# A two-block decoder on one core: low-part products one tile later, one weight split moved, sums of squares on 64 columns

## The chip, the cores and the metric

The kernel runs on one NeuronCore of a Trainium2 chip. The metric is device time in microseconds: the median over three runs of the kernel, 1620.4 us (1619.64 to 1622.11).

## What is computed

The reference takes 256 tokens `x` and 256 context tokens, each of width 1024, through two blocks of two layers.

- First block. Layer 0: RMS norm with a gain and shift from an adaptive vector (`ada`), differential attention (8 heads), residual; norm, up-projection to 2 x 2816, a depthwise convolution over three positions, SiLU gate, down-projection, residual. Tokens and context go through it, 512 rows in all. Layer 1: the same with neighbourhood attention; its FFN has the 256 tokens alone. A norm closes the block.
- Second block, two hybrid layers on the 256 tokens: a norm, one projection `w_in`, and four branches (a sparse attention with compressed keys, a pooling mixer, a short convolution, an attention with forgetting), gated and merged; a last norm.

```python
def rmsnorm(t, g):
    tf = t.astype(jnp.float32)
    tf = tf * lax.rsqrt(jnp.mean(tf * tf, axis=-1, keepdims=True) + NORM_EPS)
    return tf.astype(t.dtype) * g
...
def nsa_compress(k, pos_emb, w1, b1, w2, b2):
    ...
    blocks = k[:, idx] + pos_emb
    flat = blocks.reshape(B, nc, NSA_CMP_LEN * hd)
    return jax.nn.silu(flat @ w1 + b1) @ w2 + b2
```

## The kernel before

**Products in three parts.** Activations lie with the features on the partitions, in 8 tiles of 128 (`DT`), and 512 or 256 tokens in the free dimension. Each large product is made exact enough from split operands: an operand is a high part in the round format (`WH`, `NH`) and the low rest (`WL`, `NL`), and for each tile k of the contraction TensorE does high x high, high x low and low x high into one PSUM sum (`mm3`, L551 to L553).

**Weights.** `wstream` holds them in units of 128 x 2048. SP loads a unit into one of three `RAW` buffers; ACT copies the high part (`split_hi`, L523), in two halves; DVE, and for some second halves POOL, subtract it from the raw weights (`split_lo`, L533). All that is done two units ahead of TensorE's use: `ahead(key)` names the unit that is split while unit `key` is used. TensorE waits for the low half that holds its tile (`wait_weights`).

**Order of the work.** Each engine has one program written out by hand, as a list of steps (`pe_...`, `act_...`, `dve_...`, `pool_...`), and the engines meet at semaphores that count up. There is no scheduler: what an engine does stands in the order of the code.

**A norm** n (0 and 2 ahead of the attentions of layers 0 and 1, 1 and 3 ahead of their FFNs, 5 and 6 in the hybrid layers, 7 the last) goes like this. ACT squares a tile of `X` (L696); POOL adds the first six squares up (L716), for all norms but 0 and 5; `pe_sums` (L718 to L733) sums over the partitions: the square is the stationary operand, in groups of 128 tokens, and a column of ones `ONE` the moving one (L731). Each product is one column, the sum of squares of 128 tokens, one token per partition. In norm 5 the moving operand is the two columns of `GSQ`. One such product is two passes in the trace, as every product of plain f32. In all, 42 products have the moving `ONE` and 16 have `GSQ`, the trace's x84 and x32. DVE makes the mean (`dve_mean`, L784), POOL the root (L794), TensorE spreads it over the partitions (`pe_rs_rows`, L801), and then tile after tile: DVE scales (L828), ACT adds the shift and rounds, which is the high part (L844), and DVE (even tiles, L856) or POOL (odd tiles, after one more ACT step, L848 and L869) makes the low part. Meanwhile TensorE does products of the adaptive vectors (`pe_ada`, L565), whose 32-column stationary operands come straight from `RAW`.

**The first unit behind a norm** is where TensorE meets the normalized tiles as they come. For tile 0, `pe_high_first` (L902 to L912) does the two products with the high operand for both output halves j (L908, L909), waits for the low part, and does the third (L912). Tiles 1 to 7 then go through `pe_wide(..., abreast=True)` or, in FFN 1 where both output halves share a bank, through `pe_tiles` (L958 to L960): for each tile it waits for the low part first (`pe_wait_norm`) and then does all six products. This holds behind norms 1, 2 and 3. Norm 0 and the hybrid layers' norms have other code.

**The compression** (`pe_compress_up`, L2082 and L2083) takes two units of weights, 16 tiles each, one for keys and one for values; between them it turns the forget gates' `LF` (L2088). The low part of the first unit's first half is DVE's step `lo_prep(e, l, "kf", False)` in `dve_head`. It stands between the two parts of the rotation of the keys: `dve_turn_product` (a shuffle L1958 and a product L1960) and `dve_turn_sum` (L1967). The second halves of both units are POOL's.

Of the kernel before, what the change touches and what calls it, by code (L numbers as in the profile page):

```python
# [9 lines left out]
ALU = mybir.AluOpType  # L10
# [351 lines left out]
def bass_two_block_decoder(nc, wstream, first, small, consts, late, rpb, xin, out):  # L362
    ctx = ExitStack()
    with ctx:
# [353 lines left out]
        def pe_sums(e, n, m):  # L718
# [10 lines left out]
            width = 2 if n == 5 else 1  # L729
            for q in range(NORM_T[n] // P):  # L730
                mm = e.matmul(NB[:, width * q:width * q + width], t[:, q * P:q * P + P], GSQ[:, m, :] if n == 5 else ONE,  # L731
                              start=first and q == 0, stop=m == DT - 1, skip_group_check=True)
# [40 lines left out]
        def dve_mean(e, n):  # L773
# [4 lines left out]
            if n == 5:  # L778
                for kind in range(2):
                    mm = e.tensor_scalar(MS[:, 2 * kind:2 * kind + 2], NB[:, 0:4].rearrange("p (q s) -> p s q", s=2)[:, kind, :],  # L780
# [3 lines left out]
            e.tensor_scalar(MS[:, 0:nt], NB[:, 0:nt], 1.0 / D, EPS, ALU.mult, ALU.add).then_inc(ms_done, 1)  # L784
# [117 lines left out]
        def pe_high_first(e, n, key, outs, T, shared):  # L902
            v, wh, wl = weights(key)
            wait_weights(e, v, 0)
            e.wait_ge(n_hi, split_base(n) + NORM_T[n] // 256)
            for j, o in enumerate(outs):
                w = slice(P * j, P * j + P)
                e.matmul(o, wh[:, 0, w], NH[:, 0, 0:T], start=j == 0 or not shared, stop=False, skip_group_check=shared)  # L908
                e.matmul(o, wl[:, 0, w], NH[:, 0, 0:T], start=False, stop=False, skip_group_check=shared)  # L909
            pe_wait_norm(e, n, 0)  # L910
            for j, o in enumerate(outs):
                e.matmul(o, wh[:, 0, P * j:P * j + P], NL[:, 0, 0:T], start=False, stop=False, skip_group_check=shared)  # L912

        def pe_wide(e, key, outs, T, xh, xl, wait_x, abreast=False):
# [3 lines left out]
            if abreast:  # L918
                for k in range(1, nk):
                    wait_weights(e, v, k)  # L920
                    wait_x(k)
                    for j, o in enumerate(outs):
                        mm = mm3(e, o, wh[:, k, P * j:P * j + P], wl[:, k, P * j:P * j + P], xh[:, k, 0:T],
                                 xl[:, k, 0:T], False, k == nk - 1)
                        if k == nk - 1:
                            mm.then_inc(gemm, 1)
                return
# [2431 lines left out]
```

## Time and profile before

| | |
|---|---|
| three runs | 1619.64, 1620.4, 1622.11 us (median 1620.4) |
| the profiled execution: its own time | 1614.25 us |
| its span | 1612.1 us |
| mean granted TensorE clock | 0.996 |
| TensorE / its weight load / DVE / ACT / POOL busy | 98% / 83% / 59% / 48% / 34% |
| chain that ended last, by engine | TensorE 89%, DVE 6%, ACT 2% |
| DMA | 249.26 MB, 155 GB/s |

The profile is one execution. An engine's busy share is its time with an instruction in it; a TensorE product in it shows the time from its start to its modelled end, some 0.28 to 0.5 us, while the next may start much sooner, so the pace is read from the starts. The granted clock is the share of TensorE's full 2.4 GHz that it was given. "Idle before" with a releaser names what an engine waited for.

### The profile page before, as it was taken

The page shows a single profiled execution, that of the slowest core. Times are in us where ns is not written, and L with a number is a line of the kernel's source. Part 1 is how long each engine was busy: PE and PEld are TensorE (multiplying, and loading weights), DVE is VectorE, ACT ScalarE, POOL GpSimd, SP SyncE. Part 2 cuts the span into 40 slices and gives each one's busy share as a digit, 9 for nine tenths or more (in the row PEclk, how much of TensorE's full clock was granted, in tenths as well). Part 3 has the DMA queues.
Part 4 walks back from the last instruction along what each step waited for, and adds up shares of the span by engine and source line. Part 5 has one row for each costly group of instructions (what it writes and reads, how often), then busy time and mean ns, then how long its engine had stood idle before and what let it go on. Part 6 is the DMA issues. An engine that isn't in the chain of part 4 may idle for free.

```text
span 1612.1 us, 24595 instructions
## 1 busy us (share of the span) xinstructions
PE 1584.4 (98%) x9838; PEld 1339.2 (83%) x9838; DVE 949.9 (59%) x1485; ACT 767.5 (48%) x1410; POOL 548.8 (34%) x358
## 2 busy tenths in 40 slices
PE   8999999999999999999999999999999999999998
PEld 5778557778887888879767999999999989999987
DVE  4334485555564653343275888658776567768545
ACT  5323585444322443243274755445544555564454
POOL 2224243322211222123172111016334567533564
PEclk9999999999999999999999999999999999999999
DMA  9264500434174222364314654445534544533451
GB/s 394 83 250 186 228 9 27 183 138 164 48 282 165 83 76 81 140 209 157 104 28 163 238 187 168 169 170 183 182 131 158 183 160 170 185 128 134 180 203 58
DMA packets 52464, 249.26 MB, mean 155 GB/s; under 512 B 20608, under 2 KB 20736, under 8 KB 25856
## 3 DMA queue, kind: packets, MB, share of 16 engines
q1 hardware_dynamic: 43600, 243.90, 41.9%
q10 hardware_dynamic: 8752, 3.80, 1.0%
q8 instruction: 78, 1.28, 0.3%
q14 instruction: 34, 0.28, 0.0%
HBM read 246.63 MB, written 1.05 MB: 154 GB/s over the span
## 4 chain that ended last, share of the span: by engine, by line
PE 89%; DVE 6%; ACT 2%; issue 1%; DMA 1%; POOL 0%; SPq 0%; ACTq 0%; POOLq 0%; DVEq 0%
PE psq L551 14%; PE psq L553 14%; PE psq L552 14%; PE psq L965 7%; PE ps L551 6%; PE ps L553 6%; PE ps L552 6%; PE psq L966 4%; PE ps L965 3%; PE ps L565 2%; PE ps L966 1%; DVE WL L533 1%; PE psq L1373 1%; PE ps L1401 1%; DMA RAW<-wstream 1%
## 5 line engine op out<-in xcount | busy, mean ns | idle before, releaser
L533 POOL TENSOR_TENSOR WL<-RAW,WH 128x1024 fp32r<-128x1024 f32 (+2 forms) x116 | 304.4, 2626 | 504.5 <-ACT WH L523 493.4
L533 DVE TENSOR_TENSOR WL<-RAW,WH 128x1024 fp32r<-128x1024 f32 (+3 forms) x264 | 329.2, 1272 | 235.6 <-ACT WH L523 235.4
L523 ACT ACTIVATE WH<-RAW 128x1024 fp32r<-128x1024 f32 (+2 forms) x380 | 361.0, 1001 | 156.2 <-DMA RAW<-wstream 92.5
L551 PE MATMUL psq<-NHL,WH 128*128 128x256 f32 (+1 forms) x1260 | 410.2, 326 | 3.3 <-POOL NHL L869 1.8
L553 PE MATMUL psq<-NHL,WL 128*128 128x256 f32 (+1 forms) x1260 | 404.3, 321 | 0.0
L552 PE MATMUL psq<-NHL,WH 128*128 128x256 f32 (+1 forms) x1260 | 404.2, 321 | 0.0
L551 PEld LDWEIGHTS psq<-NHL,WH 128*128 128x128 f32 x1260 | 239.9, 190 | 32.4 <-issue 7.6
L553 PEld LDWEIGHTS psq<-NHL,WL 128*128 128x128 f32 x1260 | 239.9, 190 | 17.8
L552 PEld LDWEIGHTS psq<-NHL,WH 128*128 128x128 f32 x1260 | 240.0, 191 | 16.6
L965 PE MATMUL psq<-NHL,WH 128*128 128x512 f32 x416 | 148.6, 400 | 0.0
L551 PE MATMUL ps<-NHL,WH 128*128 128x256 f32 (+1 forms) x368 | 122.1, 332 | 0.0
L552 PE MATMUL ps<-NHL,WH 128*128 128x256 f32 (+1 forms) x368 | 121.2, 329 | 0.0
L553 PE MATMUL ps<-NHL,WL 128*128 128x256 f32 (+1 forms) x368 | 121.2, 329 | 0.0
L966 PE MATMUL psq<-NHL,WL 128*128 128x256 f32 x416 | 116.7, 280 | 0.0
L965 PEld LDWEIGHTS psq<-NHL,WH 128*128 128x128 f32 x416 | 78.2, 188 | 20.1 <-issue 0.7
L1727 DVE SCALAR_TENSOR_TENSOR TMP<-psq,SMALL,TMP 128x510 f32<-128x510 f32 (+1 forms) x64 | 39.2, 613 | 80.5 <-ACT TMP L1688 80.4
L696 ACT ACTIVATE TMP<-X 128x256 f32<-128x256 f32 (+1 forms) x52 | 25.1, 497 | 122.6 <-DVE X L1540 60.0
L1688 ACT ACTIVATE TMP<-psq,SMALL 128x512 f32<-128x512 f32 (+1 forms) x64 | 40.8, 666 | 87.7 <-PE psq L553 87.6
L966 PEld LDWEIGHTS psq<-NHL,WL 128*128 128x128 f32 x416 | 78.5, 189 | 0.0
L551 PEld LDWEIGHTS ps<-NHL,WH 128*128 128x128 f32 x368 | 69.7, 189 | 10.2 <-issue 3.3
L553 PEld LDWEIGHTS ps<-NHL,WL 128*128 128x128 f32 x368 | 69.7, 189 | 6.4
L552 PEld LDWEIGHTS ps<-NHL,WH 128*128 128x128 f32 x368 | 69.7, 190 | 6.0
(398 smaller groups left out, 2871.0 us busy)
## 6 DMA issues: line engine op xcount, KB each, us to landing
RAW<-wstream SPq DMA_DIRECT2D x196, 1024.0 KB, 4.9
RAW<-wstream SPq DMA_DIRECT2D x32, 704.0 KB, 4.0
K<-first SPq DMA_DIRECT2D x4, 1024.0 KB, 17.1
X<-xin SPq DMA_DIRECT2D x2, 1024.0 KB, 6.3
V<-first SPq DMA_DIRECT2D x2, 1024.0 KB, 19.2
Q<-first SPq DMA_DIRECT2D x2, 1024.0 KB, 25.4
BR<-rpb ACTq DMA_DIRECT2D x8, 256.0 KB, 7.9
BR<-rpb SPq DMA_DIRECT2D x8, 256.0 KB, 8.6
```

The source lines that it names most:

```text
L523: e.activation(WH[:, u % 3, a:z], RAW[:, v % 3, a:z], ACT.Copy).then_inc(w_hi, 1)
L533: e.tensor_tensor(WL[:, u % 3, a:z], RAW[:, v % 3, a:z], WH[:, u % 3, a:z].bitcast(F32), ALU.subtract).then_inc(w_lo_p if pool else w_lo_v, 1)
L551: e.matmul(o, lh, rh, start=start, stop=False)
L552: e.matmul(o, lh, rl, start=False, stop=False)
L553: return e.matmul(o, ll, rh, start=False, stop=stop)
L565: mm = e.matmul(AB[32 * j:32 * j + 32, :], CB[:, c, :], RAW[:, v % 3, 512 * j:512 * j + 512], start=k == 0, stop=k == ada_units(b) - 1)
L696: e.activation(sq_tile(n, m), X[:, m, 0:NORM_T[n]], ACT.Square).then_inc(x_sq, 1)
L965: e.matmul(o[:, 0:512], wh, x, start=start, stop=False, skip_group_check=True)
L966: return e.matmul(o[:, 0:256], wl, x[:, 0, :], start=False, stop=stop, skip_group_check=True)
L1373: e.matmul(bank[2 * (p % 2) + e2][:, :], Q[1][ps, m, qt * P:qt * P + P], K[1][ps, m, :], start=True, stop=True).then_inc(att_qk, 1)
L1688: e.activation(acc_tile(l, U, s), up_banks(l, jj)[s][:, :], ACT.Identity, scale=small_at("fconv", (3 * l + 1) * 44 + j + FT * s), bias=sma ...
L1727: e.scalar_tensor_tensor(out=a3[:, :, 1:256], in0=o3[:, :, 0:255], scalar=w(0), in1=a3[:, :, 1:256], op0=ALU.mult, op1=ALU.add).then_inc(u ...
```

## The change

Three edits, all in the order or the shape of instructions that were there.

1. `pe_high_first` now does the whole unit. For each k it does the two products with the high operand for tile k and then the one with the low operand for tile k - 1, so low parts are waited for one tile later. High parts are waited for at each tile. The number of products is the same.
2. In `dve_head`, `lo_prep(e, l, "kf", False)` stands ahead of the memset of `CM` and of `dve_turn_product`.
3. In `pe_sums`, the moving operand is 64 columns: the one column of ones read 64 times, or in norm 5 each of the two columns read 32 times. Each group of 128 tokens has its own 64 columns in PSUM, and `dve_mean` reads one of each group (one of each 32 in norm 5). Norm 0 has its own code and stays.

```diff
@@ pe_sums
-            width = 2 if n == 5 else 1
+            if n == 5:
+                kinds = GSQ[:, m, :].unsqueeze(2).to_broadcast([P, 2, 32])
+            else:
+                kinds = ONE.to_broadcast([P, 64])
             for q in range(NORM_T[n] // P):
-                mm = e.matmul(NB[:, width * q:width * q + width], t[:, q * P:q * P + P], GSQ[:, m, :] if n == 5 else ONE,
+                mm = e.matmul(NB[:, 64 * q:64 * q + 64], t[:, q * P:q * P + P], kinds,
                               start=first and q == 0, stop=m == DT - 1, skip_group_check=True)
@@ dve_mean
-                    mm = e.tensor_scalar(MS[:, 2 * kind:2 * kind + 2], NB[:, 0:4].rearrange("p (q s) -> p s q", s=2)[:, kind, :],
+                    mm = e.tensor_scalar(MS[:, 2 * kind:2 * kind + 2], NB[:, 32 * kind:32 * kind + 128:64],
-            e.tensor_scalar(MS[:, 0:nt], NB[:, 0:nt], 1.0 / D, EPS, ALU.mult, ALU.add).then_inc(ms_done, 1)
+            sums = NB[:, 0:nt] if n == 0 else NB[:, 0:64 * nt:64]
+            e.tensor_scalar(MS[:, 0:nt], sums, 1.0 / D, EPS, ALU.mult, ALU.add).then_inc(ms_done, 1)
@@ pe_high_first
+            H, base = NORM_T[n] // 256, split_base(n)
+            for k in range(DT + 1):
+                if k < DT:
+                    wait_weights(e, v, k)
+                    e.wait_ge(n_hi, base + H * k + H)
+                    for j, o in enumerate(outs):
+                        w = slice(P * j, P * j + P)
+                        e.matmul(o, wh[:, k, w], NH[:, k, 0:T], start=k == 0 and (j == 0 or not shared), stop=False,
+                                 skip_group_check=shared)
+                        e.matmul(o, wl[:, k, w], NH[:, k, 0:T], start=False, stop=False, skip_group_check=shared)
+                if k:
+                    pe_wait_norm(e, n, k - 1)
+                    for j, o in enumerate(outs):
+                        mm = e.matmul(o, wh[:, k - 1, P * j:P * j + P], NL[:, k - 1, 0:T], start=False, stop=k == DT,
+                                      skip_group_check=shared)
+                        if k == DT and (not shared or j == 1):
+                            mm.then_inc(gemm, 1)
@@ dve_head
+            lo_prep(e, l, "kf", False)
             e.memset(CM[:, 0:384].bitcast(U32), 0).then_inc(cm_zero, 1)
             dve_turn_product(e, l, 1)
-            lo_prep(e, l, "kf", False)
             dve_turn_sum(e, l, 1, KN[:, :, :])
```

How the instructions stand on TensorE around norm 1, from its last sums to the second tile of FFN 0's first unit, before (`NHL` holds `NH` and `NL`; a product names its output, the moving and the stationary tensors, and its size):

```order
L731 MATMUL ps<-ONES,TMP 128x1 x8
L565 MATMUL ps<-RAW,CB 32x512 x4
L801 MATMUL ps<-CONST,RS 128x128 x4
L565 MATMUL ps<-RAW,CB 32x512 x8
L908 MATMUL psq<-NHL,WH 128x512
L909 MATMUL psq<-NHL,WL 128x512
L908 MATMUL psq<-NHL,WH 128x512
L909 MATMUL psq<-NHL,WL 128x512
L912 MATMUL psq<-NHL,WH 128x512 x2
L551 MATMUL psq<-NHL,WH 128x512
L552 MATMUL psq<-NHL,WH 128x512
L553 MATMUL psq<-NHL,WL 128x512
```

And with the change, from the first tile's first product on (what stands ahead of it is as before but for the 64 columns of the sums):

```order
L915 MATMUL psq<-NHL,WH 128x512
L917 MATMUL psq<-NHL,WL 128x512
L915 MATMUL psq<-NHL,WH 128x512
L917 MATMUL psq<-NHL,WL 128x512
L915 MATMUL psq<-NHL,WH 128x512
L917 MATMUL psq<-NHL,WL 128x512
L915 MATMUL psq<-NHL,WH 128x512
L917 MATMUL psq<-NHL,WL 128x512
L921 MATMUL psq<-NHL,WH 128x512 x2
L915 MATMUL psq<-NHL,WH 128x512
L917 MATMUL psq<-NHL,WL 128x512
L915 MATMUL psq<-NHL,WH 128x512
```

L915 and L917 are the products of the high operand, L921 those of the low one. The low ones of the first tile now stand behind the second tile's high ones, and so on to the end of the unit.

On DVE ahead of the compression (both hybrid layers), before:

```order
L2036 TENSOR_TENSOR FHL<-TMP,FHL 128x16x16 [waits flat_hi] x2
L2038 MEMSET CM 128x384
L1958 STREAM_SHUFFLE TMP<-TMP 128x512 [waits raw_copy]
L1960 TENSOR_TENSOR TMP<-TMP,LATEC 128x512 [waits nrot_v]
L533 TENSOR_TENSOR WL<-RAW,WH 128x1024 [waits w_hi]
L1967 TENSOR_TENSOR KN<-KN,TMP 128x512 [waits nrot_c,nrot_v]
L2047 TENSOR_TENSOR LF<-TMP 128x8 [waits fx_v,fx_a]
```

With the change:

```order
L2036 TENSOR_TENSOR FHL<-TMP,FHL 128x16x16 [waits flat_hi] x2
L533 TENSOR_TENSOR WL<-RAW,WH 128x1024 [waits w_hi]
L2039 MEMSET CM 128x384
L1958 STREAM_SHUFFLE TMP<-TMP 128x512 [waits raw_copy]
L1960 TENSOR_TENSOR TMP<-TMP,LATEC 128x512 [waits nrot_v]
L1967 TENSOR_TENSOR KN<-KN,TMP 128x512 [waits nrot_c,nrot_v]
L2047 TENSOR_TENSOR LF<-TMP 128x8 [waits fx_v,fx_a]
```

L533 has moved from behind the product L1960 to a place ahead of the memset; the sum L1967 now stands directly behind the product whose semaphore it waits for.

## Rows read from the trace of the kernel before

**Rows 1.** page, section 1: busy us (share of the span) and instructions of TensorE
```profile
PE 1584.4 (98%) x9838; PEld 1339.2 (83%) x9838; DVE 949.9 (59%) x1485; ACT 767.5 (48%) x1410; POOL 548.8 (34%) x358
```

**Rows 2.** TensorE's waits: waiter <- releaser: us in total, times, longest
```profile
PE ps L2082 <- DVE WL L533: 1.8, 1, 1.8
```

**Rows 3.** timeline, TensorE, 302 to 316 us: start, us, engine, line, what, [idle before]
```profile
304.50 1.95 PE L731 MATMUL ps<-ONES,TMP 128*128 128x1 f32 x16
306.37 1.92 PE L565 MATMUL ps<-RAW,CB 128*32 128x512 f32 x8
308.22 1.92 PE L801 MATMUL ps<-CONST,RS 128*128 128x128 f32 x8
...
312.73 0.40 PE L909 MATMUL psq<-NHL,WL 128*128 128x512 f32 x1
312.96 0.63 PE L912 MATMUL psq<-NHL,WH 128*128 128x512 f32 x2
314.43 0.50 PE L551 MATMUL psq<-NHL,WH 128*128 128x512 f32 x1 [0.84 <-POOL NHL L869]
```

**Rows 4.** windows: stretch, us, busy by engine, granted TensorE clock, DMA, GB/s
```profile
308.00:309.00 1.00, 1.00 (x7) 0.78 (x4) 0.00 (x0) 0.00 (x0) 0.00 (x0) 0.50 0.72 303
...
884.00:885.00 1.00, 1.00 (x9) 0.08 (x1) 0.00 (x0) 0.00 (x0) 0.20 (x1) 0.50 0.97 410
```

**Rows 5.** timeline, TensorE, 687 to 694 us
```profile
687.12 1.06 PE L565 MATMUL ps<-RAW,CB 128*32 128x512 f32 x8
688.54 1.16 PE L801 MATMUL ps<-CONST,RS 128*128 128x128 f32 x8 [0.35 <-POOL RS L794]
...
693.98 0.51 PE L551 MATMUL psq<-NHL,WH 128*128 128x512 f32 x1 [0.96 <-POOL NHL L869]
```

**Rows 6.** timeline, TensorE, 881 to 895 us
```profile
881.71 1.50 PE L731 MATMUL ps<-ONES,TMP 128*128 128x1 f32 x12 [0.81 <-POOL TMP L716]
883.14 1.85 PE L565 MATMUL ps<-RAW,CB 128*32 128x512 f32 x8
884.92 1.23 PE L801 MATMUL ps<-CONST,RS 128*128 128x128 f32 x4
...
893.59 0.32 PE L958 MATMUL psq<-NHL,WH 128*128 128x256 f32 x1
...
894.44 1.06 PE L565 MATMUL ps<-RAW,CB 128*32 128x512 f32 x8
```

**Rows 7.** timeline, POOL's root, the second tile's high part, POOL's last low part
```profile
306.72 1.02 POOL L794 TENSOR_TENSOR RS<-MS,ONES 128x4 f32<-128x4 f32 x1 [11.80 <-DVE MS L784]
...
312.54 0.50 ACT L844 ACTIVATE NHL<-TMP,ADA 128x256 fp32r<-128x256 f32 x1
...
321.71 0.74 POOL L869 TENSOR_TENSOR NHL<-TMP,NHL 128x256 fp32r<-128x256 f32 x1 [0.20 <-ACT TMP L848]
```

**Rows 8.** timeline, POOL, 883 to 894 us: root and last low part
```profile
883.49 0.71 POOL L794 TENSOR_TENSOR RS<-MS,ONES 128x2 f32<-128x2 f32 x1 [1.83 <-DVE MS L784]
...
892.73 0.74 POOL L869 TENSOR_TENSOR NHL<-TMP,NHL 128x256 fp32r<-128x256 f32 x1 [0.72 <-ACT TMP L848]
```

**Rows 9.** timeline, DVE and POOL ahead of the second compression
```profile
1379.42 0.75 DVE L2036 TENSOR_TENSOR FHL<-TMP,FHL 128x256 fp32r<-128x256 f32 x2
...
1381.89 3.41 DVE L533 TENSOR_TENSOR WL<-RAW,WH 128x1024 fp32r<-128x1024 f32 x1
...
1381.79 2.43 POOL L533 TENSOR_TENSOR WL<-RAW,WH 128x1024 fp32r<-128x1024 f32 x1 [2.84 <-ACT WH L523]
```

**Rows 10.** timeline, DVE and POOL ahead of the first compression
```profile
1122.72 0.68 DVE L1967 TENSOR_TENSOR KN<-KN,TMP 128x512 f32<-128x512 f32 x1
...
1122.76 2.89 POOL L533 TENSOR_TENSOR WL<-RAW,WH 128x1024 fp32r<-128x1024 f32 x1 [4.12 <-ACT WH L523]
...
1126.01 3.34 POOL L533 TENSOR_TENSOR WL<-RAW,WH 128x1024 fp32r<-128x1024 f32 x1 [0.30 <-ACT WH L523]
```

**Rows 11.** timeline, TensorE, attention of hybrid layer 0: products of 64 columns
```profile
1176.78 1.90 PE L2291 MATMUL psq<-VF,TMP 128*128 128x64 f32 x16
```

More of the change, by code:

```diff
@@ L903, in pe_high_first, with pe_wide @@
             v, wh, wl = weights(key)
[L904 to L914, printed above, removed]
+            H, base = NORM_T[n] // 256, split_base(n)
[15 more added lines that the diff above has]
+                            mm.then_inc(gemm, 1)
+        def pe_wide(e, key, outs, T, xh, xl, wait_x):
             v, wh, wl = weights(key)
             nk = SHAPE[v][0]
[L918 to L927, printed above, removed]
             for j, o in enumerate(outs):
@@ L1022, in pe_qkv @@
                         pe_ada_turn(e, 5)
-                wait_x = (lambda k: pe_wait_norm(e, n, k)) if u == 0 else nothing
                 if l == 1 and i < 4:
-                    pe_wide(e, ("qkv", l, i), [bank[b][:, 0:256], bank[b][:, 256:512]], 256, NH, NL, wait_x)
+                    pe_wide(e, ("qkv", l, i), [bank[b][:, 0:256], bank[b][:, 256:512]], 256, NH, NL, nothing)
                 else:
+                    outs = [bank[b][:, :], bank[b + 1][:, :]]
                     if u == 0:
-                        pe_high_first(e, n, ("qkv", l, i), [bank[b][:, :], bank[b + 1][:, :]], 512, False)
-                    pe_wide(e, ("qkv", l, i), [bank[b][:, :], bank[b + 1][:, :]], 512, NH, NL, wait_x, u == 0)
+                        pe_high_first(e, n, ("qkv", l, i), outs, 512, False)
+                    else:
+                        pe_wide(e, ("qkv", l, i), outs, 512, NH, NL, nothing)
                 if l == 0:
@@ L1605, in pe_ffn @@
                         e.wait_ge(x_res, 16 + 4 * jj + 8)
-                    wait_x = (lambda k: pe_wait_norm(e, 1 + 2 * l, k)) if j == 0 else nothing
                     outs = [b[:, :] for b in up_banks(l, jj)]
@@ L1622, in pe_ffn @@
                     if j == 0:
-                        pe_high_first(e, 1 + 2 * l, ("up", l, j), [bank[0][:, 0:256], bank[0][:, 256:512]] if l else outs, T, l == 1)
-                    if l == 1 and j == 0:
-                        pe_tiles(e, ("up", l, j), bank[0], (0, 1), range(1, DT), NH, NL, wait_x).then_inc(gemm, 1)
+                        pe_high_first(e, 1 + 2 * l, ("up", l, j), outs, T, l == 1)
                     else:
-                        pe_wide(e, ("up", l, j), outs, T, NH, NL, wait_x, j == 0)
+                        pe_wide(e, ("up", l, j), outs, T, NH, NL, nothing)
                 pe_down(e, l, c)
```

## The prediction

> **What bounds the kernel now.** I read section 1 of the page first. TensorE is busy for 1584.4 of 1612.1 us, and no other engine is above 60% except its own weight load [rows 1]. So work on other engines costs something only where TensorE stands for it, and the change can win only TensorE's idle time or time in which its products run slowly. Next I read TensorE's waits, and then, in order of time, the stretches that the diff touches; the reader is to see in each what TensorE waits for and what it does just before.
>
> At each norm whose first unit is changed, TensorE does the first tile's six products and then stands until POOL has made the second tile's low part: 0.84 us [rows 3] and 0.96 us [rows 5]. Ahead of the second hybrid layer's compression it stands 1.8 us for a low part of the weights that DVE makes [rows 2]. And twice the clock granted to TensorE is 0.50, its lower level of 1.2 GHz [rows 4]: in the norm ahead of FFN 0, behind a run of 16 one-column passes, and in the norm ahead of FFN 1, behind 12 of them after an idle 0.81 us [rows 3, 6]. In the norm between them no such fall shows: eight passes of L565 take 1.06 us and eight of L801 1.16 us there, against 1.92 and 1.92 us in the slow stretch [rows 3, 5].
>
> The sum goes against the profiled execution (span 1612.1, its own time 1614.25 us). The median of the three runs, 1620.4 us, is 6.15 us above it; I take the saving worked out in the trace off the median, since idle time of TensorE that goes comes off either alike.
>
> **Low products one tile later.** Nothing is added: the same six products per tile, in another order. FFN 0: one product follows the other after 0.23 us (312.73 to 312.96), and the fifth slot, behind the first tile's four products of the high operand, is at 312.96 [rows 3]. Now the fifth asks for the second tile's high part, which ACT finishes at 312.54 + 0.50 = 313.04 [rows 7]: a stand of 0.1 us. Before, the six were issued by 312.96 + 2 x 0.23 = 313.42 and the next came at 314.43, a stand of 1.0 us [rows 3]. Gain 0.9. Does the wait return later? A tile takes TensorE 6 x 0.23 = 1.4 us. POOL's last low part lands at 321.71 + 0.74 = 322.45 [rows 7]. The old order needed it at the eighth tile, 314.43 + 36 x 0.23 = 322.7; the new one needs it only for its last two products, at about 313.1 + 42 x 0.23 = 322.8. It is still just in time, so the 0.9 us stay. If the high parts came a little late at each tile, 0.5 would be left; that is my lower bound, and the whole 1.0 the upper. Attention of layer 1 has the same shapes and a wait of 0.96 [rows 5]: 0.9 again. In FFN 1 the columns are half as many and TensorE is faster than the norm's chain, so the end of the unit follows POOL's last low part, 892.73 + 0.74 = 893.47 [rows 8]. Behind it stood six products, 893.59 to 894.44 [rows 6]; now two do. Gain 4/6 of 0.85 = 0.55. Together **2.35 us** (bounds 1.3 to 2.6). What is late next there is ACT's high part of each next tile.
>
> **The compression's low part ahead of the rotation.** One DVE subtraction (L533, first half of the compression's weights) moves ahead of a memset, a shuffle and a product; no DMA and no other queue moves. In the second hybrid layer it now starts when L2036 ends, at 1380.2, with POOL idle until 1381.79; it took 3.41 us because it was asked for 0.1 us after POOL's own subtraction [rows 9]; of POOL's, 1381.79 + 2.43 - 1381.89 = 2.33 us were left then, and without them it would take 1.1 us. TensorE came to stand at about 1381.89 + 3.41 - 1.8 = 1383.5 [rows 2, 9]. Even with its full 3.41 us the moved subtraction would end at 1383.6. So the wait of 1.8 goes: **1.8 us** (bounds 0 to 1.8). What is late next is the decay's LF, behind the rotation's sum; nothing there was waited for by TensorE. In the first hybrid layer TensorE did not wait at this place, so the move can gain nothing there and can only lose (second rival).
>
> A rule of the Trainium skill bears on this: SBUF — State Buffer (the part on contention on the engine side) says that a GpSimd operation and a DVE operation with two SBUF inputs take one shared pair of ports exclusively, and that whichever starts first keeps it for its whole instruction. By that rule the moved subtraction is first, takes its short time and ends near 1381.3. The row's 3.41 us beside POOL's 2.43 us fits it; the sum is 1.8 by either.
>
> **Sums of squares on 64 columns.** 58 products (116 passes) become 64 columns wide. Their own price: 16 passes of one column take 1.95 us [rows 3], 16 passes of 64 columns 1.90 us in the attention of the first hybrid layer [rows 11]. So the weight load sets the pace, and I take 0. The upper bound is the pace of the 128-column L801, 1.16 / 8 = 0.145 us apiece [rows 5], against 1.95 / 16 = 0.122: 116 x 0.023 = 2.7 us; the lower bound is 0. The mean still reads one element per token group, so DVE's operation is unchanged.
>
> What it can gain is the clock. In [rows 11] a run of 64-column passes did not bring it down, and a fall comes only behind runs of one-column passes. If the clock stays at its upper level: in the norm ahead of FFN 0, L565 is done by 306.37 + 1.06 = 307.43, the root at 306.72 + 1.02 = 307.74 [rows 3, 7], so L801 runs from 307.8 to 308.96 instead of 308.22 to 310.14: 1.2 us. L565's next products move up with it, and so does the norm's chain, which starts from L801. Ahead of FFN 1: the root is done at 883.49 + 0.71 = 884.20 [rows 8], L801 starts at 884.25 instead of 884.92 and takes half of 1.16 instead of 1.23 [rows 5, 6]: 0.67 + 0.65 = 1.3 us, which the norm's chain passes on whole. Together **2.5 us** (bounds 0 and 2.5). Nothing covers it: DVE, ACT and POOL have no part of the norm to do until L801's result is there.
>
> The Trainium skill, TensorE: Matmul & The Clock Gate, Part 1, says that the gate's ratio follows how busy the engine has been, and that being throttled is its default. It does not say that the width of a product counts. If only issue counts, one-column and 64-column passes are alike, this term is 0, and the time is that of the first rival; the row above bears more on the side of width.
>
> **Sum.** 2.35 + 1.8 + 2.5 - 0 = 6.65 us. 1620.4 - 6.65 = 1613.75, say 1613.7 us, 0.41% faster. The profiled execution would be at 1607.6.
>
> **Rivals.**
> 1. *The clock falls all the same*, at one place or both. For it: ahead of FFN 1 the fall also has 0.81 us of idling before it [rows 6], which the change leaves. Against: two shorter one-column runs with L565 between did not bring it down in the norm between. Left are 2.35 + 1.8 = 4.15 us: 1616.2; with one place of two, about 1615.0. Chance 0.27.
> 2. *POOL gets ahead of DVE in the first compression.* The rotation's sum (L1967) came at 1122.72 and POOL's subtraction at 1122.76 [rows 10]. The sum kept the lead by 0.04 us, and POOL's took 2.89 us. Now the sum stands directly behind the product it depends on and starts some 0.1 us later, behind POOL. Then LF and the second compression's low part slide behind POOL's next subtraction, asked for at 1126.01 [rows 10]. That holds DVE for some 2.4 us, the time POOL's took in [rows 9], while TensorE comes to this place at about 1127. Loss about 2.5 us: 1613.7 + 2.5 = 1616.2. It takes two close races, both of which POOL must win. By the port rule named above this is exactly what happens as soon as POOL's request is first; without a lock DVE would only be slowed. Chance 0.18.
> 3. *The gains are swallowed.* Units after the changed ones come to weights that are not ready. Against: TensorE shows no such wait anywhere but in [rows 2]. It would leave about the 1.8 of the last place: 1618.6. Chance 0.08.
> 4. *Slower: DVE late in both compressions, clock still down.* If POOL leads in both hybrid layers, each costs TensorE up to 2.8 us (POOL's 2.43 plus the waiting LF), in the second in place of the 1.8. That is 2.8 + 1.0 = 3.8 us lost against the 2.35 won by the lag: 1620.4 + 1.45 = 1621.9. It decides from the moment at which DVE asks for its second compression's low part later than POOL for its own; in the second layer DVE leads by about 0.3 us, by my reckoning from the order of its work. Chance 0.05.
>
> **How the numbers follow.** Forecast 0.42, rivals 0.27, 0.18, 0.08, 0.05. The range goes from 1612.4 (all three terms at their upper bounds, 6.9 us, and 1.1 us of scatter; the three runs lie 2.5 us apart) to 1618.8 (rival 2 without the clock: 2.35 + 1.8 - 2.5 = 1.65 saved); about 2 in 10 lie outside. About 0.2% of the time, 3.2 us, is what a measurement of this kernel can tell from no change. The forecast and rival 1 are beyond it, rival 2 mostly, rival 3 is not; taking off what scatter turns: faster 0.69, same 0.27, slower 0.04.
>
> **What would show it.** Right: no wait for POOL in the three first units but stands of at most 0.3 us for ACT's high parts; the wait of L2082 gone and DVE's subtraction there about 1.2 us long; granted clock 1.00 throughout both norms, L801's passes 1.16 us for eight. Wrong: a granted clock of 0.50 in either norm (rival 1); a new wait of the first hybrid layer's second compression near 1127, for DVE (rivals 2, 4); new waits for weights (rival 3); 64-column passes slower than 0.12 us apiece.

## The result, and the profile after

The changed kernel takes **1608.93 us** (median of 4 runs, 1608.47 to 1609.28), the kernel before beside it 1620.02 us (4 runs, 1618.73 to 1622.11): ratio 0.993, 95% interval 0.9913 to 0.9947. It is faster by 0.7%, and by more than forecast: 11.1 us saved instead of 6.65, which is below the low end of the range (1612.4).

The profiled executions tell less than half of it: 1614.25 us (span 1612.1) before, 1609.28 us (span 1607.2) after, 4.97 us apart. So the first thing to explain is why medians and profiles disagree.

Page of the changed kernel, section 1 (before: [rows 1]):

```profile
PE 1583.7 (99%) x9838; PEld 1339.1 (83%) x9838; DVE 950.6 (59%) x1485; ACT 767.6 (48%) x1410; POOL 550.2 (34%) x358
```

TensorE's waits (before: [rows 2]):

```profile
PE psq L915 <- ACT NHL L848: 1.0, 2, 0.7
PE ps L805 <- POOL RS L798: 0.7, 2, 0.4
PE ps L2082 <- DVE WL L533: 0.2, 1, 0.2
```

No first unit waits for POOL's low part (`NHL` L873) any more, and the 1.8 us ahead of the second hybrid layer's compression are gone. The 0.2 us of L2082 are another stand, in the first hybrid layer, which the kernel before does not have [rows 2]. The two waits above it are those ahead of the first tile and for the root, which the change leaves.

Timeline of TensorE at norm 1, the one ahead of FFN 0 (before: [rows 3]):

```profile
303.86 1.00 PE L734 MATMUL ps<-ONES,TMP 128*128 128x64 f32 x8
304.79 1.06 PE L565 MATMUL ps<-RAW,CB 128*32 128x512 f32 x8
305.79 2.00 PE L734 MATMUL ps<-ONES,TMP 128*128 128x64 f32 x16
307.72 1.06 PE L565 MATMUL ps<-RAW,CB 128*32 128x512 f32 x8
309.14 1.16 PE L805 MATMUL ps<-CONST,RS 128*128 128x128 f32 x8 [0.36 <-POOL RS L798]
...
312.90 0.40 PE L917 MATMUL psq<-NHL,WL 128*128 128x512 f32 x1
313.24 0.50 PE L915 MATMUL psq<-NHL,WH 128*128 128x512 f32 x1
...
322.54 1.07 PE L921 MATMUL psq<-NHL,WH 128*128 128x512 f32 x4
323.44 0.39 PE L551 MATMUL psq<-NHL,WH 128*128 128x512 f32 x1
```

Eight of L565 take 1.06 us and eight of L805 1.16 us where both took 1.92. The stand between the first tile's high products and the second's is 313.24 - 312.90 - 0.23 = 0.11 us (forecast 0.1). Sixteen passes of 64 columns take 2.00 us against 1.95 for one column. At norm 3, ahead of FFN 1 (before: [rows 6]):

```profile
880.30 1.55 PE L734 MATMUL ps<-ONES,TMP 128*128 128x64 f32 x12 [0.81 <-POOL TMP L716]
881.78 1.07 PE L565 MATMUL ps<-RAW,CB 128*32 128x512 f32 x8
882.89 0.71 PE L805 MATMUL ps<-CONST,RS 128*128 128x128 f32 x4
...
890.57 0.91 PE L921 MATMUL psq<-NHL,WH 128*128 128x256 f32 x4
891.41 1.06 PE L565 MATMUL ps<-RAW,CB 128*32 128x512 f32 x8
```

Windows over the start, norm 1, norm 3 and the compression (columns as in [rows 4]; the number behind the last count is the granted clock):

```profile
12.00:26.00 14.00, 11.31 (x76) 6.85 (x76) 6.82 (x13) 8.93 (x15) 6.52 (x5) 0.63 1.01 421
302.00:314.00 12.00, 11.64 (x80) 7.27 (x80) 4.78 (x14) 3.63 (x8) 1.95 (x3) 1.00 0.63 229
880.00:896.00 16.00, 15.36 (x118) 11.98 (x119) 10.58 (x22) 10.79 (x19) 3.91 (x6) 1.00 0.67 250
...
1388.00:1392.00 4.00, 4.00 (x35) 4.00 (x35) 2.98 (x4) 3.63 (x5) 2.34 (x1) 1.00 0.72 277
```

Both norms are at full clock. The half clock that is left is in the start; over 12 to 26 us the mean granted clock of the 14 profiles of this document goes from 0.63 to 1.00.

Timeline of DVE and POOL ahead of the second compression (before: [rows 9]):

```profile
1376.45 0.75 DVE L2036 TENSOR_TENSOR FHL<-TMP,FHL 128x256 fp32r<-128x256 f32 x2
1377.12 1.21 DVE L533 TENSOR_TENSOR WL<-RAW,WH 128x1024 fp32r<-128x1024 f32 x1
...
1378.82 2.40 POOL L533 TENSOR_TENSOR WL<-RAW,WH 128x1024 fp32r<-128x1024 f32 x1 [2.84 <-ACT WH L523]
```

In the second layer the moved subtraction takes 1.21 us and is done at 1378.33, 2.2 us before TensorE's first product of the compression at 1380.52. The same ahead of the first compression (before: [rows 10]):

```profile
1119.76 2.86 DVE L1967 TENSOR_TENSOR KN<-KN,TMP 128x512 f32<-128x512 f32 x1
1122.55 0.39 DVE L2047 TENSOR_TENSOR LF<-TMP 128x8 f32<-128x8 f32 x4
...
1122.93 4.52 DVE L533 TENSOR_TENSOR WL<-RAW,WH 128x1024 fp32r<-128x1024 f32 x2
...
1119.68 2.39 POOL L533 TENSOR_TENSOR WL<-RAW,WH 128x1024 fp32r<-128x1024 f32 x1 [4.11 <-ACT WH L523]
...
1122.92 3.45 POOL L533 TENSOR_TENSOR WL<-RAW,WH 128x1024 fp32r<-128x1024 f32 x1 [0.78 <-ACT WH L523]
```

Here POOL is now 0.08 us ahead of the sum L1967, which takes 2.86 instead of 0.68 us. In exchange the LF behind it takes 0.39 us, where in the kernel before, in the same stretch of DVE's timeline, LF was the one that ran beside POOL:

```profile
1123.32 2.59 DVE L2047 TENSOR_TENSOR LF<-TMP 128x8 f32<-128x8 f32 x4
1125.83 0.17 DVE L2049 TENSOR_SCALAR CM<-CM 128x24 f32<-128x24 f32 x1
1125.91 4.53 DVE L533 TENSOR_TENSOR WL<-RAW,WH 128x1024 fp32r<-128x1024 f32 x2
```

So DVE reaches the second compression's low part 3.17 us after the sum's start, where it was 3.19, and the pair takes as long as before (4.52 and 4.53 us). TensorE stands 0.18 us there:

```profile
1124.20 0.33 PE L2082 MATMUL ps<-WH,FHL 128*128 128x128 f32 x1 [0.18 <-DVE WL L533]
```

### The profile page after: what moved, and what is told of

It reads as the page before. It is cut to its first block, busy times and chain, and to the rows that moved or that the text cites. A ratio compares the mean times of both kernels' runs of the same rounds, so it can differ in the third digit from the quotient of the medians.

```text
span 1607.2 us, 24595 instructions
## 1 busy us (share of the span) xinstructions
PE 1583.7 (99%) x9838; PEld 1339.1 (83%) x9838; DVE 950.6 (59%) x1485; ACT 767.6 (48%) x1410; POOL 550.2 (34%) x358
## 4 chain that ended last, share of the span: by engine, by line
PE 91%; DVE 5%; ACT 1%; issue 1%; DMA 1%; POOL 0%; SPq 0%; POOLq 0%; ACTq 0%; DVEq 0%
PE psq L551 14%; PE psq L553 14%; PE psq L552 14%; PE psq L967 7%; PE ps L551 6%; PE ps L553 6%; PE ps L552 6%; PE psq L968 4%; PE ps L967 3%; PE ps L565 2%; PE ps L968 1%; PE psq L1376 1%; PE ps L1404 1%; PE psq L2291 1%; PE ps L1391 1%
## 5 line engine op out<-in xcount | busy, mean ns | idle before, releaser
L533 POOL TENSOR_TENSOR WL<-RAW,WH 128x1024 fp32r<-128x1024 f32 (+2 forms) x116 | 303.8, 2621 | 508.8 <-ACT WH L523 497.8
L533 DVE TENSOR_TENSOR WL<-RAW,WH 128x1024 fp32r<-128x1024 f32 (+3 forms) x264 | 328.8, 1270 | 232.0 <-ACT WH L523 231.8
L551 PE MATMUL psq<-NHL,WH 128*128 128x256 f32 (+1 forms) x1232 | 399.1, 324 | 1.0 <-ACT TMP L1086 0.5
L553 PE MATMUL psq<-NHL,WL 128*128 128x256 f32 (+1 forms) x1232 | 393.4, 319 | 0.0
L552 PE MATMUL psq<-NHL,WH 128*128 128x256 f32 (+1 forms) x1232 | 393.3, 319 | 0.0
L551 PEld LDWEIGHTS psq<-NHL,WH 128*128 128x128 f32 x1232 | 234.6, 190 | 27.9 <-issue 7.0
L553 PEld LDWEIGHTS psq<-NHL,WL 128*128 128x128 f32 x1232 | 234.6, 190 | 16.7
L552 PEld LDWEIGHTS psq<-NHL,WH 128*128 128x128 f32 x1232 | 234.8, 191 | 15.7
L967 PEld LDWEIGHTS psq<-NHL,WH 128*128 128x128 f32 x416 | 78.2, 188 | 20.1 <-issue 0.7
L968 PEld LDWEIGHTS psq<-NHL,WL 128*128 128x128 f32 x416 | 78.6, 189 | 0.0
```

The lines of the kernel that those rows point to most:

```text
L533: e.tensor_tensor(WL[:, u % 3, a:z], RAW[:, v % 3, a:z], WH[:, u % 3, a:z].bitcast(F32), ALU.subtract).then_inc(w_lo_p if pool else w_lo_v, 1)
L551: e.matmul(o, lh, rh, start=start, stop=False)
L552: e.matmul(o, lh, rl, start=False, stop=False)
L553: return e.matmul(o, ll, rh, start=False, stop=stop)
L967: e.matmul(o[:, 0:512], wh, x, start=start, stop=False, skip_group_check=True)
L968: return e.matmul(o[:, 0:256], wl, x[:, 0, :], start=False, stop=stop, skip_group_check=True)
```

## Experiments

Runs 1 to 4 share a chip, as do 5 to 8 and 9 to 12. The kernel before ran beside each four: 1616.90 us (31 runs, 1612.44 to 1623.74), 1620.01 (17, 1614.22 to 1624.94) and 1619.17 (25, 1612.84 to 1624.44). Ratios below are to these, with their 95% interval. Each run also left the profile of one execution.

**1. The kernel before, once more.** No edit. It asks what an execution other than the profiled one looks like.

> The kernel before, unchanged, to see the granted clock of more than one of its executions. The change saved 11.1 us in the medians (1620.0 to 1608.9), but only 4.97 us between the two profiled executions (1614.25 to 1609.28), and the profiled execution of before lay 6 us under its median. Theory C (clock): the usual execution of before holds more half-clock time at the norms than the profiled one did, so an execution near 1620 us shows a mean granted clock below 0.996, about 0.990 to 0.993, and further stretches at 0.50 in or near the norms. Theory S (structure): the clock is the same 0.996 in an execution of 1620 us, and the 6 us lie in waits or transfers instead.

1619.52 us (12 runs, 1613.94 to 1621.74), ratio 1.0014 (0.9998 to 1.0031). The executions fall into two groups with a thin middle: of the 31 beside it, 15 lie from 1612.4 to 1615.7 us, at mean granted clocks of 0.995 to 0.997, and the others, from 1616.9 to 1623.7, at 0.989 to 0.994. The profiled one here is of the upper group (1621.26 us, span 1619.1). Its timeline of TensorE at the second compression, and windows from there on:

```profile
1386.07 0.30 PE L2082 MATMUL ps<-WH,FHL 128*128 128x128 f32 x1 [1.80 <-DVE WL L533]
...
1387.88 0.27 PE L2082 MATMUL ps<-WH,FHL 128*128 128x128 f32 x1
1387.99 0.28 PE L2083 MATMUL ps<-WL,FHL 128*128 128x128 f32 x1
...
1388.66 0.41 PE L2083 MATMUL ps<-WL,FHL 128*128 128x128 f32 x1
1388.88 0.41 PE L2082 MATMUL ps<-WH,FHL 128*128 128x128 f32 x1
1389.09 0.41 PE L2083 MATMUL ps<-WL,FHL 128*128 128x128 f32 x1
...
1401.48 0.41 PE L551 MATMUL psq<-NHL,WH 128*128 128x256 f32 x1
1401.70 0.34 PE L552 MATMUL psq<-NHL,WH 128*128 128x256 f32 x1
1401.88 0.28 PE L553 MATMUL psq<-NHL,WL 128*128 128x256 f32 x1
```

```profile
1384.00:1388.00 4.00, 2.20 (x21) 2.03 (x19) 4.00 (x9) 2.49 (x3) 1.97 (x3) 1.00 0.24 53
1388.00:1392.00 4.00, 4.00 (x23) 4.00 (x22) 1.48 (x3) 0.27 (x1) 3.40 (x1) 0.52 0.99 387
1392.00:1396.00 4.00, 4.00 (x20) 4.00 (x21) 2.55 (x5) 3.58 (x6) 0.00 (x0) 0.50 0.90 346
1396.00:1400.00 4.00, 4.00 (x21) 4.00 (x21) 0.85 (x2) 1.78 (x4) 2.45 (x1) 0.50 0.12 20
1400.00:1404.00 4.00, 4.00 (x28) 4.00 (x28) 0.89 (x1) 0.58 (x1) 2.48 (x1) 0.77 0.62 246
```

Some 2 us behind the end of the 1.8 us stand the products step from 0.11 us apart (1387.88, 1387.99) to 0.21 (1388.66, 1388.88, 1389.09) and stay there until 1401.7: 13.5 us at the lower level, 1.2 GHz, half of it lost, some 6.7 us. Of the four profiles with this stand empty (the kernel before, runs 1 to 3) three show the fall, 2.0, 1.5 and 0.7 us behind the stand; the one that the prediction was made from is the fourth. The time from the L565 behind norm 3 (894.44 us [rows 6]) to the end, in which the compression lies, measures it a second way: 717.66 us in the profile predicted from, 724.36 here, 6.70 more. Of the expectation's two theories the clock one holds, but the place is the compression, not the norms: both norms are at full clock here.

**2. The wide sums alone** (the hunks of `pe_sums` and `dve_mean`).

```diff
...
+                kinds = ONE.to_broadcast([P, 64])
...
-                mm = e.matmul(NB[:, width * q:width * q + width], t[:, q * P:q * P + P], GSQ[:, m, :] if n == 5 else ONE,
+                mm = e.matmul(NB[:, 64 * q:64 * q + 64], t[:, q * P:q * P + P], kinds,
...
```

> Only the sums of squares on 64 columns. Theory C: it takes away the half-clock stretches of every execution, so it carries 2.5 us by my sum plus the 4.4 us that the forecast missed: about 6.9 us saved, 1613.1 us, with a granted clock of 1.00 at norms 1, 2 and 3. Theory S: it carries no more than my 2.5 us, 1617.5 us, and the missing 4.4 us are in one of the other two edits.

1619.40 us (7 runs, 1617.74 to 1620.01), ratio 1.0022 (1.0006 to 1.0037): no gain, and neither of the two times expected. The compression's 1.8 us wait is there, and behind it the half clock (0.57 over 1386 to 1402 us). All seven executions lie in the upper group, against 16 of the 31 beside it and eight of 12 in run 1. Whether the wide sums make the upper group more frequent can't be told from seven.

**3. The lag alone** (the hunk of `pe_high_first`).

```diff
-            pe_wait_norm(e, n, 0)
...
+                if k:
+                    pe_wait_norm(e, n, k - 1)
```

> Only the low-part products one tile later (sums on one column, compression as before). Theory C: my 2.35 us, 1617.7 us, with the granted clock still falling to 0.50 at norms 1 and 3. Theory S with the lag as the cause: 2.35 + 4.4 = 6.8 us, 1613.2 us.

1619.41 us (12 runs, 1611.18 to 1620.35), ratio 1.0009 (0.9991 to 1.0027). Three executions at 1611.18 to 1611.47, the other nine from 1617.95 on, with nothing between. POOL's waits are gone, and yet the median does not move, where 1617.7 or 1613.2 us were expected: the upper group hides it. The three lie 1.0 to 1.3 us under the lowest of the 31 of the kernel before.

**4. The compression's low part alone** (the hunk of `dve_head`).

```diff
+            lo_prep(e, l, "kf", False)
             e.memset(CM[:, 0:384].bitcast(U32), 0).then_inc(cm_zero, 1)
             dve_turn_product(e, l, 1)
-            lo_prep(e, l, "kf", False)
```

> Only the compression's low part ahead of the rotation. Both theories: 1.8 us or a little less, 1618.2 us, if the first hybrid layer stays without a wait; theory S with this edit as the cause: 1.8 + 4.4 = 6.2 us, 1613.8 us. If POOL gets ahead of DVE in the first compression (my second rival): a new wait of about 2.5 us near 1127 us and no gain.

1612.03 us (11 runs, 1610.72 to 1613.74), ratio 0.9975 (0.9962 to 0.9988). The upper group is gone; the compression runs at full clock. The expectation had 1618.2 us for the wait alone. Against the median beside it this is 4.9 us, against run 1's 7.5 us, for a wait of 1.8.

**5. Eight constant products in the stand.** The kernel before, its wait untouched, with products of constants of 256 columns ahead of the second compression. Nobody reads their results: they go to the bank in which the compression's own products start anew.

```diff
+            for _ in range(8 * l):
+                e.matmul(bank[6][:, 0:256], IDENT, const_at("s2", 0, 256), start=True, stop=True)
```

> The kernel before, with eight products of constants put on TensorE where it waits 1.8 us ahead of the second hybrid layer's compression; they are written where the compression's first product overwrites them. The wait itself stays: DVE's low part is as late as before. Theory I (idling lowers the clock): what cost the usual execution of before some 6.8 us was half clock through the compression's products (0.214 us apiece instead of 0.112), set off by this wait. With TensorE busy there the clock stays at 1.00 and the times lie together as in e3_cmp, about 1.8 us above it: 1613.8 us. Rival W (the compression's own thin products lower the clock, whatever stands ahead): half-clock executions near 1620 us remain, and the median is like that of before, 1617 to 1620 us.

1615.75 us (12 runs, 1614.29 to 1617.44), ratio 0.9974 (0.9962 to 0.9986). The fill runs for 3.27 us (1382.76 to the compression's first product at 1386.03), longer than the stand that it fills, and still wins: the wait is not what costs most, the clock behind it is. Of the 17 executions beside it 13 lie at 1619.5 us or above, of these 12 none is above 1617.44, and in the profile both norm 3 and the compression are at full clock. So the rival, that the compression's own products lower the clock whatever stands ahead, does not hold.

**6. The lag and the compression, without the wide sums** (diffs of 3 and 4).

> The change without its wide sums. If the wide sums matter only where the clock falls at norms 1 and 3, which the profiles of e0 and e3 did not show and those of before and e2 did: e3_cmp's 1612.0 less my 2.35 us for the lag, 1609.7 us, with single executions up to 2.5 us longer; after minus this is the worth of the wide sums, 0 to 1 us in the median. If my forecast of 2.5 us for the clock holds in every execution: 1611.4 us.

1610.14 us (6 runs, 1608.98 to 1611.94), ratio 0.9940 (0.9924 to 0.9956); 1609.7 was expected if the clock at the norms counts only where it falls, 1611.4 if it counts in every execution.

**7. The wide sums and the compression, without the lag** (diffs of 2 and 4).

> The change without the lag: 1608.9 + 2.35 = 1611.3 us if the lag is worth what I summed; 1608.9 us if the norm's high parts hold TensorE back instead of the low ones. Its profile shows the waits for POOL of 0.84 and 0.96 us again, and the granted clock 1.00 at all norms.

1611.06 us (6 runs, 1610.04 to 1611.87), ratio 0.9947 (0.9929 to 0.9964), against 1611.3 expected.

**8. The change again, beside 5 to 7.**

> The changed kernel again, beside the same executions of the kernel before: 1608.9 us, all executions within 1 us of it, none near 1615 or above, mean clock 0.996 to 0.997.

1610.02 us (6 runs, 1609.37 to 1611.10), ratio 0.9940 (0.9923 to 0.9956). By medians the wide sums are worth 0.1 us (1610.14 - 1610.02) and the lag 1.0 (1611.06 - 1610.02). The profile of 7 had full clock in the start, that of 8 had 0.63, and the third run of L642 came at 29.39 in the one and at 30.82 in the other: differences of 1 us between medians of six are partly the start's.

**9. Four constant products in the stand.**

```diff
+            for _ in range(4 * l):
+                e.matmul(bank[6][:, 0:256], IDENT, const_at("s2", 0, 256), start=True, stop=True)
```

> The kernel before with four constant products of 256 columns (some 1.6 us by the 3.27 us that eight took) in TensorE's 1.8 us ahead of the second hybrid layer's compression; the wait for the low weights stays. Theory (idling of TensorE drops the clock for the compression): executions close together at 1613 to 1615 us, median near 1614.2, i.e. 1.5 us under the run with eight, whose products ended 1.5 us behind the stand; none at 1618 or above. Rival (eight products helped because they were many and dense, four are too few): the scatter of 1612 to 1624 us stays, median near 1619.

1613.01 us (12 runs, 1612.80 to 1614.78), ratio 0.9968 (0.9950 to 0.9985). Of the 25 executions of the kernel before beside it, 17 lie above 1616.8 us; of these 12, none. The fill begins when TensorE gets there, and the compression's first product comes at 1385.29 us, against 1385.44 in the profile of the kernel before:

```profile
1383.43 1.89 PE L2078 MATMUL ps<-LATEC,CONST 128*128 128x256 f32 x8
1385.29 0.33 PE L2084 MATMUL ps<-WH,FHL 128*128 128x128 f32 x1
```

The wait is still paid. 6.2 us of the median go all the same.

**10. The same stand filled with eight products of one column.**

```diff
+            for _ in range(8 * l):
+                e.matmul(bank[6][:, 0:1], IDENT, const_at("s2", 0, 1), start=True, stop=True)
```

> The same place filled with eight products of one column (16 passes, some 1.9 us by the 0.12 us of a one-column pass of the sums of squares). It tells whether not idling is enough or whether the columns count. If being busy is enough: as with the four wide ones, 1613 to 1615 us, median near 1614.3, no half clock behind the stand. If thin work counts as idleness: the scatter of before stays, median near 1619, half clock from about 1386 to 1400 us.

Timeline of TensorE there:

```profile
1383.89 1.84 PE L2078 MATMUL ps<-LATEC,CONST 128*128 128x1 f32 x16
1385.75 0.33 PE L2084 MATMUL ps<-WH,FHL 128*128 128x128 f32 x1
```

1616.84 us (12 runs, 1613.88 to 1623.66), ratio 0.9993 (0.9975 to 1.0012). Both theories of the expectation are too clean: five executions lie from 1613.9 to 1615.1, seven from 1616.8 on. Seven of 12 against 17 of 25 without a fill can't be told apart; against none of 12 with four wide products it can. TensorE was issuing all through the stand, and it did not hold the clock as the four wide products did. The profiled execution is one of the five and had full clock at the compression.

**11. The change with a filled start.** Constant products of 256 columns in TensorE's waits of the start.

```diff
+                if j < 2:
+                    pe_constant(e, bank[0], 256)
                 pe_first_sel(e, j)
                 if j == 0:
                     pe_rs_rows(e, 0)
+                    for _ in range(3):
+                        pe_constant(e, bank[0], 256)
```

> The changed kernel with constant products also in the start (three of 256 columns behind the first rotation rows, one ahead of each of the first two selections), where the changed kernel's profile shows half clock from 15 to 25 us. If the half clock there costs time: 1 to 1.5 us faster than the changed kernel of this call (near 1608.7 if that is at 1610.0) and full clock in the start. Rival (the start is set by the arriving weights, of which the chain of the profile gives 37.9% of the first 30 us, so that TensorE's clock is hidden there, as in the change without the lag, whose start ran at full clock for no gain): the same as the changed kernel, within 0.5 us; or slower by the 1.5 us or so that the fillers take.

**12. The change, beside it.**

> The change once more, for the comparison with the filled start on the same chip. 1609 to 1610 us, executions within 2 us of each other, clock 0.996.

1607.81 us with the fill (6 runs, 1607.24 to 1608.66), ratio 0.9932 (0.9906 to 0.9958); 1608.56 us without (8 runs, 1607.53 to 1611.77), ratio 0.9940 (0.9919 to 0.9961). The executions of run 12 lie 4.2 us apart, where 2 were expected. The start of the filled one is at full clock:

```profile
12.00:26.00 14.00, 12.04 (x98) 8.32 (x98) 8.06 (x15) 8.90 (x15) 6.52 (x5) 1.00 1.02 422
```

and its third run of L642 comes at 28.78 us against 30.16 in run 12 and 30.65 in the changed kernel's first profile. It has the lowest median here, by 0.75 us where 1 to 1.5 were expected, with ranges that overlap. The rival that the arriving weights hide the start's clock falls by the 1.4 us at the mark, and by the same mark in all 14 profiles: 28.78 to 29.39 us in the three with full clock over 12 to 26 us, 29.47 and 29.73 in the two with 0.88, 30.00 to 32.28 in the nine with 0.63 to 0.77. That the median shows half of it fits executions in which the start is fast anyway, which was not measured.

**The norms' clock over all 14 profiles.** Mean granted clock in four stretches, from windows of each:

```
                      sums      12:26  302:314  880:896  1386:1402
before                1 col      0.88    0.86     0.89     1.00
run 1 (before again)  1 col      0.77    1.00     1.00     0.57
run 2 wide            64 col     0.76    1.00     1.00     0.57
run 3 lag             1 col      0.63    0.86     1.00     0.53
run 4 compression     1 col      0.76    1.00     1.00     1.00
run 5 fill 8          1 col      0.76    1.00     1.00     1.00
run 6 lag+compr.      1 col      0.76    0.86     1.00     1.00
run 7 wide+compr.     64 col     1.00    1.00     1.00     1.00
run 8 change          64 col     0.63    1.00     1.00     1.00
run 9 fill 4          1 col      1.00    0.86     0.89     1.00
run 10 fill thin      1 col      0.88    0.86     0.89     1.00
run 11 filled start   64 col     1.00    1.00     1.00     1.00
run 12 change         64 col     0.76    1.00     1.00     1.00
after                 64 col     0.63    1.00     1.00     1.00
```

Norm 1 falls in five of eight profiles with one-column sums and in none of six with wide ones; norm 3 in three of eight and none of six. Run 9's windows show it as the kernel before had it:

```profile
302.00:314.00 12.00, 11.15 (x73) 6.41 (x71) 5.42 (x15) 4.27 (x10) 2.49 (x3) 0.86 0.64 231
880.00:896.00 16.00, 14.28 (x102) 9.80 (x96) 9.30 (x21) 10.51 (x19) 4.67 (x7) 0.89 0.67 258
```

That speaks for the wide sums, but another cause has to be kept apart, the moment at which the norm comes. With one-column sums, norm 1 falls in all five profiles whose first sums start at 302.19 to 303.76 us and in none of the three in which they start at 304.18 to 305.29. The six with wide sums start at 302.35 to 303.86, in or just behind the range that falls, so there the width is what differs. At norm 3 the three falls have their sums at 881.26 to 882.03; of the wide ones only run 2, at 881.85, lies in that range, and the others come at 879.11 to 880.55, as run 6 does with one-column sums and without a fall. So at norm 3 the change may have escaped by being early, and the width is not shown. In time no run isolates it either: runs 6 and 8 differ by 0.1 us in the median.

Norm 3 and the compression also go together. In the five profiles with no wide fill in the stand and the old order of the weight split, the clock falls either at norm 3 (before, run 10) or behind the stand (runs 1 to 3), never at both.

## Why the prediction was right, and where it failed

The prediction was wrong: 11.1 us went where it had 6.65, and the time lies below its range. The step that failed is the compression's term. It priced the stand at its own 1.8 us and nothing behind it; in the usual execution the stand also sets off 6.7 us of half clock, so the term is 8.5. The clock term at the norms erred the other way, 2.5 us forecast and 0.1 found in the median (runs 6 and 8).

Measure from marks that every profile has: the third run of L642 (29.47 us before, 32.28 in run 1, 30.65 after), the first sums of norm 1 (302.62, 305.29, 303.86), of norm 2 (684.27, 685.73, 683.60), the sums behind the 0.81 us wait in norm 3 (881.71 [rows 6], 883.19, 880.30), the next unit's L565 (894.44 [rows 6], 894.74, 891.41), the end of the span.

```profile
30.65 1.07 PE L642 MATMUL ps<-V,CB 128*32 128x256 f32 x16
...
683.60 1.00 PE L734 MATMUL ps<-ONES,TMP 128*128 128x64 f32 x8
```

```
stretch               before   run 1    after     saved of    saved of  forecast for it
                                                  before      run 1
L642 to norm 1        273.15   273.01   273.21    -0.06       -0.20     0
norm 1 to norm 2      381.65   380.44   379.74     1.91        0.70     lag 0.9 + clock 1.2
norm 2 to norm 3      197.44   197.46   196.70     0.74        0.76     lag 0.9
norm 3 to next L565    12.73    11.55    11.11     1.62        0.44     lag 0.55 + clock 1.3
L565 to the end       717.66   724.36   715.79     1.87        8.57     wait 1.8
sum                  1582.63  1586.82  1576.55     6.08       10.27     6.65
```

Against the execution predicted from, the sum held to 0.6 us. That the spans differ by only 4.9 is the start: it took 1.2 us longer in the execution profiled after. Against run 1, an execution of the upper group, it did not: the two norms' clock gives nothing and the last stretch gives 8.57 us, the 1.8 of the wait and 6.7 of clock. Runs 2 and 3, with the stand empty, take 724.36 and 725.60 us there; the seven profiles with the moved subtraction take 715.39 to 716.14. Point by point:

- **The lag, 2.35 us: right, 2.25.** Between runs 7 and 8, which differ in the lag alone, norm 1 to norm 2 goes from 380.60 to 379.70, norm 2 to norm 3 from 197.60 to 196.75, norm 3 to L565 from 11.61 to 11.12: 0.9, 0.85 and 0.5 us against 0.9, 0.9 and 0.55. The order of medians (1.0 us) agrees in sign and is blurred by the start.
- **The compression's wait, 1.8 us: the step that failed.** The wait went as described, the subtraction took 1.21 us against 1.2. But the step priced the wait alone. I took its cost from an execution in which the clock stayed up behind it. In about half of the 31 executions beside run 1, and in 17 of the 25 beside run 9, the time is that of the upper group; in the three profiles of that group (runs 1 to 3) the clock falls, in run 1 for some 13 us, and 6.7 us more are lost. Removing the stand removes both: run 4 shows it alone, and run 9 shows that the loss hangs on the stand being empty, since with the wait paid in full and four wide products in it 6.2 us of the median go.
- **"I take the saving off the median, since idle time of TensorE that goes comes off either alike": the sentence behind it.** The median lay 6.15 us above the profiled execution. I named this gap and did not ask what it was made of. It was the same size as what the change would take away besides. Lag 2.25, wait 1.8 and clock behind the stand 6.7 make 10.75 of the 11.1 us; this is a sum of terms from single profiles, and the medians of run 1 and run 4 give 7.5 for the last two.
- **The clock at norms 1 and 3, 2.5 us: right in size where it occurs, wrong in how often.** Norm 1 to norm 2 takes 381.61 in run 9 with the fall and 380.48 in run 4 without it: 1.1 us against 1.2. Norm 3 to L565 takes 12.73 us in the kernel before with the fall and 11.55 in run 1 without it: 1.2 against 1.3. Yet norm 3 fell in three of eight profiles only, so the median holds a part at most, and runs 6 and 8 find 0.1 us. Runs 1, 4 and 5, whose norms stayed up, had slow starts, with the third L642 at 31.2 to 32.3 us against 29.1 to 29.7 in those where both norms fell: the two losses take turns, which may be why neither shows in a median. That was not tested.
- **"Twice the clock is 0.50", and "a fall comes only behind runs of one-column passes": misread.** The trace predicted from has a third stretch, in the start: the granted clock is 0.50 over 20 to 22 us and 0.88 over 12 to 26. The last one-column passes, eight of L760, had started at 11.71 us; TensorE had stood idle for 1.50 and 0.58 us just before the fall, with short runs of products between. A fall behind idling was thus on record, and the 1.8 us stand should have been asked the same question.
- **The price of wide sums, 0: nearly.** 2.00 against 1.95 us for 16 passes, 0.05 x 116 / 16 = 0.4 us over all; run 2 is inside its neighbours' scatter at 1619.40.
- **Rival 1** (clock falls all the same) did not come in any of the six profiles with wide sums. **Rival 2** did come as far as its race: POOL won it by 0.08 us, and the sum took 2.86 us. The forecast loss of 2.5 us was 0.18 at most, because in the kernel before LF had lost the same race one instruction later (2.59 us), which [rows 10] does not show. **Rivals 3 and 4** did not occur.

The rule of the Trainium skill on the port pair that DVE and GpSimd share (SBUF — State Buffer, section "SBUF: two separate sides"), that the one that starts first keeps it for its whole instruction, agrees with the traces: the moved subtraction takes 1.21 us with POOL idle, and the sum takes 2.86 us where the 2.31 us that were left of POOL's instruction and its own 0.68 make 2.99. The Trainium skill, TensorE: Matmul & The Clock Gate, Part 1, says that the number of products that run at the lower clock at the start of one kernel differs from run to run. The starts agree: over 12 to 26 us the changed kernel's three profiles have 0.63, 0.63 and 0.76, the kernel before 0.88 and 0.77. That the same holds in the middle of a kernel is what the two groups of the 31 executions show.

## What to carry to other kernels

When the median lies further from the profiled execution than the runs of a quiet kernel scatter (here 6 us, with the granted clock of single runs from 0.989 to 0.997), the profile may show one of two ways the kernel runs, and the cost of a wait must be asked of both. Price a stand of TensorE with what it does to the clock of the work behind it; here that was a long run of 128-column products. A cheap test of it is to put constant products into the stand: if the scatter goes while the wait stays, the clock was the cost. Sort the single runs before trusting a median: a small gain (run 3) can vanish under two groups.

## What the hardware showed that I had not expected

- A stand of 1.8 us with 128-column products behind it can bring the granted clock to 0.50, and it stays there for 13.5 us of unbroken issue, through 128-column products and into the 256-column ones behind them (run 1). The same stand left the clock alone in the kernel before's first profile and, by their times, in 15 of the 31 executions beside run 1.
- Not standing idle was not enough here: 16 one-column passes in the stand left seven of 12 executions in the upper group, four products of 256 columns none of 12 (runs 9 and 10). Norm 1 points the same way: with one-column sums the clock fell in five of eight profiles, with 64-column sums, at the same pace (2.00 against 1.95 us for 16 passes), in none of six. At norm 3 the moment of the norm is a rival that no run excludes.
- A fall in the start, from 15 to 25 us, costs 1.4 us at the third L642 (30.16 against 28.78) although the weights are still arriving there, at 421 GB/s over 12 to 26 us of the changed kernel.
